# Leaving out TensorE's filler products while the tokens are routed, in a two-layer hybrid decoder with a mixture of experts

## The reference

```python
group_prob = softmax(x2 @ w_r1 + b_r1)              # 4 groups, the best one is taken
fine = (x2 @ w_r2 + b_r2).reshape(n_tok, 4, 8)      # 8 experts in each group
ev, ei = top_k(fine of the chosen group, 2)         # two experts for each token
gates = gp * softmax(ev)
hid = silu(x @ w_gate[e]) * (x @ w_up[e])           # each expert, on its own tokens
y = hid @ w_down[e]                                 # times the gate, added into the token's row
```

## Time and profile before

| | |
|---|---|
| median of 3 runs | 1651.03 us (1650.68 to 1652.24) |
| the profiled execution | 1649.66 us |
| its span, first to last instruction | 1647.9 us |
| mean granted clock of TensorE | 0.994 of full |
| PE busy | 1609.4 us (98%) |
| filler products in it | 108, 269 to 277 ns each, overlapping |

### The profile page before, as it was taken

One profiled execution on the slowest core, in us unless ns is written; L12 is line 12 of the kernel. 1 busy time (PEld: TensorE's weight loads), 2 busy tenths in 40 slices (PEclk: granted clock), 3 DMA queues, 4 the chain that ended last, 5 costly groups with the idle time before them and its releaser, 6 DMA issues.

```text
span 1647.9 us, 23231 instructions
## 1 busy us (share of the span) xinstructions
PE 1609.4 (98%) x9692; PEld 1012.5 (61%) x9699; DVE 786.8 (48%) x1321; ACT 337.4 (20%) x563; POOL 144.4 (9%) x140
## 2 busy tenths in 40 slices
PE   8999999999999999989999999999999999999998
PEld 6876686555544555457887887888655554455554
DVE  4899845334333333435553354555533433334343
ACT  4225542101010101033222222232210101010112
POOL 0030001111110111000000000000111111011100
PEclk9999999999999999999999999999999999999999
DMA  8212148999999999984222132126799999999995
GB/s 311 103 52 103 43 181 345 423 422 422 421 424 424 424 423 423 425 330 153 71 83 103 52 103 101 53 103 253 299 422 424 421 421 423 425 422 423 423 424 230
DMA packets 67852, 474.94 MB, mean 288 GB/s; under 512 B 8720, under 2 KB 21056, under 8 KB 41760
## 3 DMA queue, kind: packets, MB, share of 16 engines
q1 hardware_dynamic: 58528, 455.10, 67.6%
q10 hardware_dynamic: 3072, 10.18, 1.6%
q0 software_dynamic: 6144, 8.13, 1.4%
HBM read 475.75 MB, written 6.29 MB: 293 GB/s over the span
## 4 chain that ended last, share of the span: by engine, by line
PE 84%; DMA 7%; DVE 6%; ACT 2%; issue 1%; DVEq 0%; SPq 0%; ACTq 0%
PE psum L960 26%; PE psum L992 12%; PE psum L872 10%; PE psum L874 10%; PE psum L873 10%; PE psum L1106 7%; DMA in_uT<-in_expert_w_up 2%; DMA in_pair<-in_expert_w_up 2%; DVE xs L1896 2%; PE psum L974 2%; DMA raw<-in_odd_w_in 2%; PE psum L983 1%; DVE w_lo L697 1%; PE psum L1324 1%; PE psum L1005 1%
## 5 line engine op out<-in xcount | busy, mean ns | idle before, releaser
L2264 DVE TENSOR_TENSOR h<-h,psum 128x512 f32<-128x512 f32 x240 | 154.2, 684 | 226.3 <-PE psum L1106 226.3
L2514 POOL DMA_INDIRECT x_e<-xs_dram,quarter_of x128 | 128.2, 1002 | 1330.8 <-DVE quarter_of L2198 659.7
L697 DVE TENSOR_TENSOR w_lo<-raw,w_hi 128x2048 fp32r<-128x2048 f32 x46 | 105.4, 2291 | 171.8 <-ACT w_hi L691 171.8
L691 ACT ACTIVATE w_hi<-raw 128x2048 fp32r<-128x2048 f32 x46 | 88.1, 1915 | 305.0 <-PE psum L874 303.9
L992 PE MATMUL psum<-raw,hidT 128*64 128x512 f32 x640 | 145.3, 596 | 0.1
L872 PE MATMUL psum<-w_hi,uT_hi 128*128 128x512 f32 x352 | 139.6, 397 | 3.4 <-DVE h L2388 1.4
L2243 DVE SCALAR_TENSOR_TENSOR y_lo<-psum,rt,y_hi 128x512 fp32r<-128x512 f32 x66 | 49.2, 748 | 193.0 <-ACT y_hi L1666 193.0
L874 PE MATMUL psum<-w_lo,uT_hi 128*128 128x512 f32 x352 | 137.8, 391 | 0.0
L873 PE MATMUL psum<-w_hi,uT_lo 128*128 128x512 f32 x352 | 137.7, 391 | 0.0
L1666 ACT ACTIVATE y_hi<-psum,rt 128x512 fp32r<-128x512 f32 x62 | 42.6, 687 | 388.0 <-PE psum L1106 289.1
L1106 PE MATMUL psum<-y_hi,to_token 64*128 64x512 f32 (+1 forms) x464 | 106.6, 445 | 6.6 <-DVE y_lo L2243 6.6
(11 more groups left out here) (276 smaller groups left out, 2442.8 us busy)
## 6 DMA issues: line engine op xcount, KB each, us to landing
raw<-in_expert_w_down SPq DMA_DIRECT2D x38, 2048.0 KB, 30.8
raw<-in_expert_w_up SPq DMA_DIRECT2D x20, 2048.0 KB, 30.2
free_b<-in_expert_w_gate SPq DMA_DIRECT2D x20, 2048.0 KB, 29.7
in_pair<-in_expert_w_down SPq DMA_DIRECT2D x20, 2048.0 KB, 30.3
in_pair<-in_expert_w_up SPq DMA_DIRECT2D x20, 2048.0 KB, 30.4
in_uT<-in_expert_w_up SPq DMA_DIRECT2D x20, 2048.0 KB, 29.9
xs<-in_expert_w_gate SPq DMA_DIRECT2D x20, 2048.0 KB, 28.3
free_a<-in_expert_w_gate SPq DMA_DIRECT2D x18, 2048.0 KB, 30.3
```

What stands on the lines that cost most here:

```text
L691: nc.scalar.activation(part(w_hi[half]), half_of(n, half, by_columns), ACT.Copy).then_inc(hi_ok[half], 1)
L697: nc.vector.tensor_tensor(part(w_lo[half]), half_of(n, half, by_columns), part(w_hi[half]).bitcast(F32), ALU.subtract).then_inc(lo_ok[half ...
L2264: ins = V.tensor_tensor(dst, dst, psum[:, SUM_BANKS[half]], ALU.add)
L2514: G.indirect_dma_start(x_e[:, b, s], None, xs_quarters, bass.IndirectOffsetOnAxis(ap=quarter_of[:, s, e:e + 1], axis=0), bounds_check=4 * ...
```

## The change

Both numbers of the tuple become zero. `warm` then issues nothing, in both layers; all waits stay where they are. Nothing reads what the removed products wrote.

```diff
-WARM = (46, 8)
+WARM = (0, 0)
```

## The result

The changed kernel takes **1656.3 us** (median of 7 runs, 1655.29 to 1657.35); the kernel of before, run beside it, 1650.75 us. The ratio is **1.0036**, with a 95% interval of 1.0026 to 1.0046, that is +5.9 us (4.3 to 7.6); the medians differ by 5.6. The forecast was +4.5 us, 1655.5 us, within 1652.0 to 1659.0. The profiled execution took 1657.13 us with a span of 1655.3 us, against 1649.66 and 1647.9.

What follows compares the result with a forecast made beforehand. Each layer's expert loop was taken to be bound by its weight stream, whose start waits for PE in the routing. Terms of +2.25 us a layer, +4.5 us in both, on 1651.03 gave 1655.5 us, range 1652.0 to 1659.0.

Steps and rivals of the forecast that it cites:

- The place and the mechanism: In both routings PE's rest of 5.65 us lowers the clock; slower direct rows delay the weight stream and each layer's end.
- rival "not slower": In the routings the clock holds or the ring absorbs expert 0's delay: -0.2 us, 1650.8 us; clean case 12%.
- The third rival: PE's rest speeds DVE's routing chain or lands weights earlier: 1647 us or less; chance under 3%.
- Term 1: Ahead of the direct rows, removing the 8 fillers lets these start earlier: -0.1 us a layer.
- Term 2: The 14 counting products ahead of the direct rows run at the low clock: +0.35 us a layer, bounds 0 and +0.51.
- Term 3: Direct rows run at the low clock for 4.3 us, losing 0.465 each: +2.0 us a layer, bounds 1.0 and 3.05.
- The sum per layer: All terms together delay each layer's routing, and so its end, by +2.25 us, bounds +0.9 and +3.5.
- The rival of the late clock: Clock stays low through direct rows, table, turning and half the gate matrix: 12.4 us in all, 1663.4 us; chance 10%.

Runs made afterwards that it cites:

- kernel with 46 alone: Kernel of before without the 8 fillers, the 46 kept; ratio 1.0002; its profile ran some 40 us late from the attention stage on.
- the one with 28: Kernel of before with 20 more fillers added to the 8 ahead of the direct rows, the 46 kept; ratio 1.0021.

## Why the prediction was right

**The place and the mechanism** held. The rest of 5.65 us became 5.73 us, the clock fell in it in every profile without the 46, and in the routing nothing but the direct rows paid noticeably. The kernel with 46 alone shows that the 8 have no part; the one with 28 shows that a delay there reaches the end, since the weight stream can't make it up. Both parts of the rival "not slower" are thereby gone: the clock does not hold, and the delay is not hidden. The third rival, that the rest frees something, did not come either: from the start of DVE's first operation (L2049) to that of its last (L2072) it is 5.26 us in layer 0, before and after.

**The terms, for one layer:**

- Term 1, the 8 fillers: forecast -0.1, measured 0.0. `oh_direct` releases the direct rows 0.15 us after its end and not 0.06, so that in the kernel of before too they could not have started earlier than at 260.14.
- Term 2, the counting products at the low level: forecast +0.35, measured +0.02 (from their start to the direct rows 1.40 against 1.38 us). Thin products hardly lengthen. Unforeseen, PE took up work 0.15 us after `both` instead of 0.06, +0.09. Terms 1 and 2 were to make +0.25 and made +0.11; the direct rows started later by that and not more.
- Term 3: forecast 4.3 us x 0.465 = 2.0. Measured in the changed kernel's own profile 5.2 and 3.6 us, mean 4.4, with the direct rows and what follows up to the gate matrix 2.55 and 1.75 us longer, mean 2.15. That is 0.49 per low microsecond. The price of 0.465 was read from products whose operand is 128 columns wide; the direct rows, with 64, lost slightly more, and why is not shown. An estimate by the Trainium skill's formulas (TensorE: Matmul & The Clock Gate, "Back-to-back issue gap") is 0.494; the trace, with 0.49, agrees with that better than with my row.
- The sum per layer: forecast +2.25. Over nine routings without any filler (both layers of the changed kernel's profile, of its repetition and of its two single executions, and layer 0 of the kernel that keeps layer 1's) it lies from +1.75 to +2.66, mean +2.18. That the mean comes so near is in part luck: terms 1 and 2 came out 0.14 too high and term 3 slightly too low, and the 4.3 us were the mean of three unlike places, while the low part of the direct rows ran from 3.4 to 5.2 us.

**The rival of the late clock** did not come: the clock was back inside the direct rows in all nine.

**What the forecast lacked.** The measured +5.9 us lie above the routings' 4.1 to 4.6 us; the interval's lower end, +4.3, just reaches them. What remains, some 1 to 2 us, stood in no term. In the first profile the kernel's start gave 2.6 us more. That start varies by 2 us between executions of the kernel of before as well (251.9, 252.0 and 254.0), with the arrival of the first rows and the clock there. But all five profiles of kernels that lack the 46 in both layers have L900 between 253.9 and 254.7 us, and of the eight others (the one with the shifted attention left out) only one reaches that (251.9 to 254.0). The first turning separates them without exception.

The times of whole executions say the same. Of 74 of the kernel of before 47 took less than 1650.4 us. If the change added only the 4.6 us of the routings, about two in three of the changed kernel's should lie under 1655.0; of its 14 none does (the lowest is 1655.07). With 0 and 8 fillers two of six do. So chance is an unlikely account of the changed kernel's excess, and the late first turning goes with the programs that have no filler ahead of `chosen` in either layer. How is open. I know of no path from instructions of the routing to the first 20 us.

## What to carry to other kernels

Work that nobody reads can be worth its place where TensorE waits for a chain of small operations just ahead of products that set the end: here it kept the clock at 2.4 GHz for them. Price a rest by the products behind it, about 0.49 us for each microsecond that they run at 1.2 GHz, and only if they are on the path; a rest of 3.4 us at the end of layer 0, with the same fall of the clock, cost nothing. Fill the rest whole: with 23 or 35 of the 46 fillers left, 1.5 to 1.7 us of the 2.2 us that a layer's routing lost was there already. In the whole time these two kernels lost 2.5 and 2.6 us, the changed one 5.9; their logits were not late (251.9 and 252.0 us).

## What the runs showed of the hardware that was not expected

- Rests far shorter than the 3.3 us of the rows brought the clock down: 1.83 and 0.87 us with 0.5 us of 32-column products between them in both layers, and a single 1.78 us in some executions and not in others. 0.63 and 0.87 us did not.
- The length of a rest does not decide alone. Ahead of the first turning a rest of 2.27 us (46 and 28 fillers) was followed by the low level and one of 2.56 us (0 and 8 fillers) was not. The windows of the two:

```profile
9.10:11.80 2.70, 2.70 (x11) 1.59 (x11) 2.59 (x4) 2.63 (x8) 0.00 (x0) 0.50 1.06 364
```

```profile
8.50:15.00 6.50, 5.45 (x36) 4.00 (x37) 5.82 (x9) 5.59 (x12) 0.00 (x0) 1.00 1.08 363
```

- A shorter rest does not spare in proportion. With 5.7 us a layer's routing lost 1.75 to 2.66 us, with 3.1 us 1.68, with 1.8 us 1.54: in the latter two the clock fell only about when the direct rows began, and stayed low for 3.2 to 3.4 us of them.
- The 14 counting products took 0.02 us longer at half the clock.
- PE took up work 0.15 us after `both` had ended behind a rest of 5.7 us, and 0.05 to 0.06 us after it behind rests of 0.63, 1.83 and 3.13 us.
